# Context's projections in half as long pieces, a shorter recurrence chunk, and their phases at other gathers

## What is computed

```python
def peer_ffn(x, wq, sub_keys, u, v):           # 8 heads, top 16 of 128 x 128 experts each
    ...
        s1, i1 = lax.top_k(sc[:, :, 0], PEER_TOPK)
        s2, i2 = lax.top_k(sc[:, :, 1], PEER_TOPK)
    ...
        top_s, pos = lax.top_k(cand, PEER_TOPK)
        eidx = jnp.take_along_axis(cidx, pos, axis=-1)
        g = jax.nn.softmax(top_s, axis=-1)
        a = jax.nn.gelu(jnp.einsum('chkd,cd->chk', jnp.take(u, eidx, axis=0), xc), approximate=False)
        return jnp.einsum('chk,chkd->cd', (g * a), jnp.take(v, eidx, axis=0))
```

```python
def _gdn_scan(q, k, v, log_a, beta, s0):       # 4 heads, chunks of 128
    g = jnp.cumsum(log_a..., axis=-1)
    rel = g[..., :, None] - g[..., None, :]
    a = einsum(kc, kc) * bc * jnp.where(strict, jnp.exp(rel), 0.0)        # bc is beta
    rhs = jnp.concatenate([bc * vc, bc * jnp.exp(g)[..., None] * kc], axis=-1)
    u, wk = split(triangular_solve(a + I, rhs))
    k_tail = kc * jnp.exp(g_last - g)
    v_new = u - wk @ s;  s_next = exp(g_last) * s + k_tail^T @ v_new
    if q is not None: o = (qk * exp(rel) where incl) @ v_new + (q * exp(g)) @ s_prev
```

## Time and profile before

| | |
|---|---|
| time, median of 3 runs | 2995.73 us (2994.79 to 2996.75) |
| the profiled execution | 2992.89 us, span 2991.1 us, mean granted clock of PE 0.918 |
| busy: PE | 2436.7 us, 81% of the span |
| busy: DVE | 1598.9 us, 53% |
| busy: ACT, POOL | 836.0 us and 830.9 us, 28% each |
| gathers of the second layer | 1147 to 1890 us |
| x's features and recurrence | 1890 to 2250 us |

### The profile page before, as it was taken

How to read it: one execution, slowest core, us unless ns; L and a number is a source line. 1 busy time by engine, 2 the same in 40 slices (tenths; PEclk the granted TensorE clock), 3 DMA queues, 4 the chain that set the end, 5 groups by cost and what they waited for, 6 DMA issues and landing times.

```text
span 2991.1 us, 29479 instructions
## 1 busy us (share of the span) xinstructions
PE 2436.7 (81%) x9692; PEld 1331.3 (45%) x9692; DVE 1598.9 (53%) x3289; ACT 836.0 (28%) x2272; POOL 830.9 (28%) x723
## 2 busy tenths in 40 slices
PE   7898888888887988998897899789797786767673
PEld 3684333333333766344443455458783532222221
DVE  4556657485444636758889877556644521121111
ACT  1313333333332412343343444323110111111110
POOL 1004333343331102334444556112010112122221
PEclk9799999999999799999999999899998788888887
DMA  7029999999998126999898899612113399999994
GB/s 276 1 85 403 422 422 422 422 415 422 422 398 346 57 85 248 376 366 395 355 420 313 358 422 395 245 43 71 43 57 131 140 408 397 389 391 381 382 381 147
DMA packets 129843, 885.95 MB, mean 296 GB/s; under 512 B 23184, under 2 KB 23568, under 8 KB 31760
## 3 DMA queue, kind: packets, MB, share of 16 engines
q0 software_dynamic: 86976, 553.74, 46.0%
q1 hardware_dynamic: 42704, 330.22, 27.5%
HBM read 877.56 MB, written 37.75 MB: 306 GB/s over the span
## 4 chain that ended last, share of the span: by engine, by line
PE 46%; DMA 25%; DVE 20%; ACT 4%; issue 3%; SPq 1%; POOL 1%; DVEq 0%; ACTq 0%; POOLq 0%
PE ps L155 44%; DMA ring<-in_peer_uv,idx_u 11%; DMA ring<-in_w_gu 6%; DVE ring L1307 6%; DVE arena L76 5%; DMA ring<-in_w_down 3%; ACT arena L125 3%; PE ps L158 2%; DMA arena<-in_w_gu 2%; DMA arena<-in_w_down 1%; DVE arena L1307 1%; DVE iu L113 1%; DVE arena L109 1%; SPq L2560 1%; DVE arena L97 1%
## 5 line engine op out<-in xcount | busy, mean ns | idle before, releaser
L155 PE MATMUL ps<-ring,arena 128*128 128x512 f32 (+3 forms) x3264 | 1262.9, 653 | 281.2 <-ACT arena L125 159.9
L155 PEld LDWEIGHTS ps<-ring,arena 128*128 128x128 f32 (+2 forms) x3264 | 473.6, 180 | 957.3 <-issue 605.1
L1307 DVE CUSTOM_DVE_ANT_0 ring<-ring,h 128x1024 f32<-128x1024 f32 x448 | 563.0, 1257 | 328.3 <-DMA ring<-in_peer_uv,idx_u 294.9
L2377 POOL DMA_INDIRECT ring<-in_peer_uv,idx_u x448 | 491.5, 1097 | 754.8 <-PE ps L155 609.4
L155 PE MATMUL ps<-arena 128*128 128x128 f32 (+7 forms) x2504 | 502.8, 383 | 106.4 <-ACT arena L125 42.9
L125 ACT ACTIVATE arena<-arena 128x1 f32<-128x1 f32 (+4 forms) x1097 | 296.7, 270 | 747.6 <-DVE arena L1307 646.3
L155 PEld LDWEIGHTS ps<-arena 128*128 128x128 f32 (+3 forms) x2504 | 316.0, 193 | 263.5 <-issue 148.3
L76 DVE TENSOR_TENSOR arena<-arena,ps 128x512 f32<-128x512 f32 (+1 forms) x158 | 93.7, 593 | 446.9 <-ACT arena L125 358.6
L125 ACT ACTIVATE arena<-ps 128x512 f32<-128x512 f32 (+4 forms) x198 | 109.8, 554 | 774.1 <-PE ps L155 712.5
L155 PE MATMUL ps<-ring,hT 128*128 128x512 f32 (+2 forms) x896 | 307.0, 503 | 16.9 <-DVE hT L97 11.9
L125 ACT ACTIVATE arena<-cst,arena 128x128 f32<-128x128 f32 x512 | 205.5, 401 | 162.3 <-PE ps L155 122.0
(11 more groups left out here) (117 smaller groups left out, 1486.6 us busy)
## 6 DMA issues: line engine op xcount, KB each, us to landing
ring<-in_w_gu SPq DMA_DIRECT2D x98, 1024.0 KB, 28.5
ring<-in_w_down SPq DMA_DIRECT2D x52, 1024.0 KB, 29.8
ring<-in_w_in SPq DMA_DIRECT2D x16, 2048.0 KB, 12.6
arena<-in_w_gu SPq DMA_DIRECT2D x30, 1024.0 KB
ring<-in_w_mod SPq DMA_DIRECT2D x12, 2048.0 KB
ring<-in_peer_wq SPq DMA_DIRECT2D x8, 2048.0 KB, 8.1
ring<-in_w_o SPq DMA_DIRECT2D x6, 2048.0 KB, 11.1
ring<-in_w_gates SPq DMA_DIRECT2D x12, 1024.0 KB, 4.9
```

The costliest lines, as they stand in the source:

```text
L155: return self.e.matmul(o, lhsT, rhs, start=start, stop=stop, skip_group_check=True)
L1307: v.done(v.e.tensor_tensor_reduce(out=row, in0=row, in1=h[:, n // 128, :], scale=1.0, scalar=0.0, op0=ALU.mult, op1=ALU.add, accum_out=aa[ ...
L2377: g.e.indirect_dma_start(out=landing(n), out_offset=None, in_=d["peer_uv"], in_offset=bass.IndirectOffsetOnAxis(ap=idx_u[:, n:n + 1], axis ...
```

## The change

In words:

- `beside`: the phases of the second layer stand at n = 6, 8, ... 128, at 11, 21, ... 121, and at 139, 141, ... 237; 124 of them.
- `rows_mm` for the context's `Rk` and `Rv` yields after 4 matmuls instead of 8, and PE's `conv_features` yields in the middle of each of its two pieces. The other engines' generators have as many idle phases more.
- `gdn_chunk`: DT is made for x alone, and its product with the triangle stands behind level 2. ACT multiplies kk by beta as it copies it out of PSUM, in four operations (one a head) behind the exp of Dm, where one copied it before; DVE's product of Am with beta is gone. rk takes one product instead of two (with gc times beta, four columns) and stands behind level 1. In the tail PE waits for rv before U, where it waited for rk.

```diff
@@ -201,7 +201,7 @@
 def beside(l, n):
 
     if l:
-        return 1 if n in range(10, 130, 2) or n in range(138, 250, 2) else 0
+        return 1 if n in range(6, 130, 2) or n in range(139, 239, 2) or n in range(11, 131, 10) else 0
     return 1 if n in range(12, 246, 9) else 0
@@ -655,7 +655,7 @@
                     if name == "Rv" and not s.x:
                         yield from idle(2)
                     yield from rows_mm((s.tag, name), xT, R(area, 4), 512, ("loaded", s.tag, name), *ready,
-                                       among=among)
+                                       grain=8 if s.x else 4, among=among)
@@ -682,6 +682,8 @@
                             for k in range(8):
                                 t = pe.mm(b[:, (m - m0) * 256:(m - m0) * 256 + 256],
                                           w[:, k * 512 + m * P:k * 512 + (m + 1) * P], xT[:, k, :], k == 0, k == 7)
+                            if m == m0 and not s.x:
+                                yield
                         pe.done(t, ("ps", s.tag, name, m0), *([("used", s.tag, name)] if m0 else []))
                         yield
@@ -733,7 +735,7 @@
                     yield
                 rv, rk, kt = Dm, Am, Xm
                 b = fresh(*g, "U", among=among)
-                pe.wait_ge(*at(*g, "rk"))
+                pe.wait_ge(*at(*g, "rv"))
                 heads_mm(b, lambda sl, hd: [(XT[:, sl], rv[:, sl])], ("ps", *g, "U"))
                 b2 = fresh(*g, "W", among=among)
                 heads_mm(b2, lambda sl, hd: [(rk[:, sl], XT[:, sl])], ("ps", *g, "W"))
@@ -1377,7 +1379,7 @@
                     v.ts(xn[:, c, :], src[:, c, :], rs[:, c:c + 1], None, ALU.mult, None, (tag, c))
 
             def row_features(s):
-                yield from idle(3 * len(s.row_blocks) + (0 if s.x else 2))
+                yield from idle(3 * len(s.row_blocks) + (0 if s.x else 6))
@@ -1415,7 +1417,7 @@
                 rw = raw.rearrange("p (m t) -> p m t", m=4)
                 cvv = cv.rearrange("p (m t) -> p m t", m=4)
                 for a, name, area, f0 in kinds:
-                    for _ in range(3):
+                    for _ in range(3 if s.x else 5):
                         yield
@@ -1467,6 +1469,8 @@
                 bec = be[:, c, dr * 4:dr * 4 + 4]
                 ck = slice(c * P, (c + 1) * P)
                 g = (s.tag, dr, c)
+                Gk, Gv = s.GG[:, 0, c, :], s.GG[:, 1, c, :]
+                rv, rk, kt = Dm, Am, Xm
@@ -1476,20 +1480,17 @@
                 for hd in range(4):
                     sl = slice(hd * P, (hd + 1) * P)
                     v.ts(Dm[:, sl], GR[:, sl], gc[:, hd:hd + 1], 0.0, ALU.subtract, ALU.max, (*g, "D"))
-                for hd in range(4):
-                    sl = slice(hd * P, (hd + 1) * P)
-                    v.ts(DT[:, sl], GR[:, sl], gc[:, hd:hd + 1], 0.0, ALU.subtract, ALU.min)
+                if s.x:
+                    for hd in range(4):
+                        sl = slice(hd * P, (hd + 1) * P)
+                        v.ts(DT[:, sl], GR[:, sl], gc[:, hd:hd + 1], 0.0, ALU.subtract, ALU.min)
                 yield
                 v.wait_ge(*at(*g, "exp D"))
-                v.wait_ge(*at(s.tag, "beta", c))
                 v.tt(heads(Dm, 4), heads(Dm, 4), bc(strict, 1, 4), ALU.mult)
                 v.wait_ge(*at("out", *g, "kk"))
-                v.tt(Am, kk, Dm, ALU.mult)
-                v.tt(heads(Am, 4), heads(Am, 4), bc(bec, 2, P), ALU.mult, (*g, "A"))
-                v.wait_ge(*at(*g, "exps"))
-                v.tt(heads(DT, 4), heads(DT, 4), bc(tri, 1, 4), ALU.mult)
+                v.tt(Am, kk, Dm, ALU.mult, (*g, "A"))
                 I4 = bc(ident, 1, 4)
                 v.tt(heads(Xm, 4), heads(Am, 4), bc(C("lvl0"), 1, 4), ALU.mult)
                 v.tt(heads(Xm, 4), I4, heads(Xm, 4), ALU.subtract)
@@ -1505,11 +1506,13 @@
                         v.tt(Xm, Xm, tile_of(*g, "dX", lv)[:, :], ALU.subtract, ("out", *g, "dX", lv))
                     v.wait_ge(*at("ps", *g, "dXT", lv))
                     v.tt(XT, XT, tile_of(*g, "dXT", lv)[:, :], ALU.subtract, ("out", *g, "dXT", lv), (*g, "X", lv + 1))
-                Gk, Gv = s.GG[:, 0, c, :], s.GG[:, 1, c, :]
-                rv, rk, kt = Dm, Am, Xm
-                v.tt(heads(rv, 4), heads(Gv, 4), bc(bec, 2, P), ALU.mult)
-                v.tt(heads(rk, 4), heads(Gk, 4), bc(bec, 2, P), ALU.mult)
-                v.tt(heads(rk, 4), heads(rk, 4), bc(gc, 2, P), ALU.mult, (*g, "rk"))
+                    if lv == 1:
+                        v.wait_ge(*at(*g, "exps"))
+                        v.tt(gc, gc, bec, ALU.mult)
+                        v.tt(heads(rk, 4), heads(Gk, 4), bc(gc, 2, P), ALU.mult)
+                    if lv == 2 and s.x:
+                        v.tt(heads(DT, 4), heads(DT, 4), bc(tri, 1, 4), ALU.mult)
+                v.tt(heads(rv, 4), heads(Gv, 4), bc(bec, 2, P), ALU.mult, (*g, "rv"))
                 v.tt(heads(kt, 4), heads(Gk, 4), bc(ekt, 2, P), ALU.mult)
                 if s.x:
                     v.tt(heads(qe, 4), heads(qe, 4), s.GqT[:, :, ck], ALU.mult)
@@ -2075,7 +2078,7 @@
 
             def row_features(s):
                 for name, i, _ in s.row_blocks:
-                    yield from idle(5 if i and not s.x else 3)
+                    yield from idle(3 if s.x else 7 if i else 5)
                     X = s.Rk if name == "Rk" else s.Rv if name == "Rv" else s.Rq
@@ -2135,12 +2138,16 @@
                 gc, eg, ekt = smalls3
                 g = (s.tag, dr, c)
                 yield
-                take(kk, *g, "kk")
                 a.wait_ge(*at(*g, "D"))
                 a.act(Dm, Dm, ACT.Exp, (*g, "exp D"), scale=-1.0)
+                a.wait_ge(*at("ps", *g, "kk"))
+                for hd in range(4):
+                    a.act(kk[:, hd * P:(hd + 1) * P], tile_of(*g, "kk")[:, hd * P:(hd + 1) * P], ACT.Copy, ("out", *g, "kk"),
+                          scale=be[:, c, dr * 4 + hd:dr * 4 + hd + 1])
                 last = heads(GR, 4)[:, :, end:end + 1].rearrange("p h x -> p (h x)")
                 a.wait_ge(*at(*g, "ekt"))
-                a.act(DT, DT, ACT.Exp)
+                if s.x:
+                    a.act(DT, DT, ACT.Exp)
                 a.act(ekt, ekt, ACT.Exp)
                 a.act(eg, last, ACT.Exp)
                 a.act(gc, gc, ACT.Exp, (*g, "exps"))
@@ -2412,7 +2419,7 @@
 
             def conv_features(s, kinds, lane):
                 for a, name, area, f0 in kinds:
-                    for _ in range(6):
+                    for _ in range(6 if s.x else 8):
                         yield
```

## The result

The changed kernel takes **3006.68 us** (median of 7 runs, 3004.80 to 3009.45) against 2995.73 us before (7 runs): a ratio of 1.0039, 95% interval 1.0028 to 1.0050. The forecast was 2971 us with a range of 2948 to 2991: the time went the other way, to near the rival that ended slower (3012). The profiled execution took 3006.68 us, its span is 3004.9 us.

The account below looks back on a forecast made before the run. The prediction took DMA holes in the second layer's gathers, opened by late PE or DVE, as the prize. Gather stage -16 and x's recurrence -8.5, about -25 us, gave 2971 us, range 2948 to 2991.

Parts of the forecast that it names:

- What bounds the stage: Second layer's gathers: PE or DVE late by more than eight gathers opens DMA holes, never made up, 70 us in all.
- The term for the half pieces: Projections: each block's PE work spreads over more gathers, 0.76 us of lag draining per extra gather; -8 us.
- the slower rival: Gathers: twelve phases at odd gathers each stop the DMA 3.45 us, price 41 us, total 3012 us; chance 0.13.
- deciding price of 2.6 us: Gathers: cost per odd phase from which the slower rival decides, (25 + 6) / 12.
- Projections: -8: Projections before the first front: DMA loss shrinks by 8 us of 23.0, bounds 0 and 12.6.
- Fronts: -2.7 us each: Each chunk's front: DVE loses four subtractions (1.3 us) and two products (0.69 each), -2.7 us.
- Chunk 1: +3: First chunk's front and levels: topk and front packed into six gathers, then six phases in ten; +3 us, bounds -2.7 and +8.
- Chunk 2: -9: Second chunk's front moves to gathers 118 to 123, free of routing, ahead of the norm; -9 us, bounds 0 and -14.5.
- The prediction's own sign of being wrong in the main: Gathers: chunk 2's hole keeps its size, or holes appear at each of gathers 21, 31 and so on.
- Chunk 3: +1.4: Third chunk's front moves to gathers 163 to 169 beside three 1.4 us routing pieces: 4.1 - 2.7 = +1.4 us.
- Chunk 4: -3.2: Fourth chunk's front: DVE's excess falls from 3.9 to 1.2 us, worth -3.2 us.
- x's recurrence: -8.5: x's recurrence, after the gathers: shorter PE waits before U and A, less 1.1 for slowed rk; -8.5 us, bounds -11 and -3.
- the price of rk in level 1: x's recurrence, level 1: DVE's rk operations slow beside POOL, +0.4 us each, 1.1 us in the sum.

Follow-up runs that it names:

- no_odd: Changed kernel without phases at odd gathers before 130 (positions 2, 4, ... 128, 131, 138, 140, ... 254): 2983.8 us, 0.9962 of the kernel before.
- shifted: no_odd with twelve phases one gather earlier (11, 21, ... 121 instead of 12, 22, ... 122): 2984.0 us.
- dt_only: Kernel before, with DT left out for the context's chunks and the wait for "exps" moved to the tail: 2989.8 us, ratio 0.9986.
- pos_only: Changed kernel with the old gdn_chunk, keeping the half pieces, idle phases and 124 positions: 3013.4 us, 1.0062 of the kernel before.
- even_dt_rk: no_odd with kk as before (one ACT copy, beta's product on DVE): 2979.5 us, 0.9954 of the kernel before.
- alg_early: alg_only with its 116 positions moved up to 2, 4, ... 128 and 138, 140, ... 240: 2994.4 us.
- alg_only: Changed kernel with the new gdn_chunk, but the old projections' pieces, idle phases and 116 positions: 2985.3 us, 0.9968 of the kernel before.
- dt_rk: alg_only with kk as before (one ACT copy ahead of the exp, beta's product on DVE): 2983.9 us, 0.9972 of the kernel before.

## Why the prediction was wrong, point by point

- **What bounds the stage** was right: DMA holes where PE or DVE is late, none of them made up. Sized that way they account for the loss (+14.0 against +13.6 us).
- **The step that failed is the price of the extra phases, which the sum put at nothing in the projections.** The term for the half pieces lets every block drain over more gathers, and the sum has nothing for the odd phases that take that room back. What dismissed them was the slower rival's "Against it". It took "from 1470 to 1550 PE was busy for 77 of 80 us and the DMA never stopped" as a sign that an extra phase can hide. The row says the reverse: PE had 3 us to spare in 80. More phases ahead of gather 130 have no room in such a stretch. The changed kernel has 74 phases there, before had 60 and no_odd 64. Between no_odd and the change each of the twelve odd phases costs 1.7 us of the stage, in part by the place that it gives front 3; the rival had 3.45. Its deciding price of 2.6 us rested on a gain of 25; the rest of the change was worth 11 (no_odd), so the point was 0.9. The rival had the direction right. That its 3012 lies near 3006.7 is luck: a price twice too high was set against a gain twice too high. Its mechanism, three engines going round in one gather beside neighbours, is not shown: with a neighbour on one side and no added work there was no cost (`shifted`).
- **Projections: -8 was +4.1.** The term counted the gathers over which each block is spread. But from the first phase to the front there were 82 gathers before and 82 after, with PE 221.3 and 223.4 us busy: what the blocks gained, the room between them lost. In no_odd, where there are 98, the projections give -5.2.
- **Fronts: -2.7 us each.** For DT alone, 2.0 of the 2.7, this was right in size in the profile: the four chunks gain 8.2 us in dt_only, though the whole time gains 4.4. The 0.69 for kk's product did not come: that edit gave 0.7 us in four fronts alone, and seemed to cost 2.3 beside the others.
- **Chunk 1: +3 was +4.3**, inside its bounds, by the mechanism named: too many phases in ten gathers. The term added up PE's work over the gathers in this one place, and the projections needed the same sum.
- **Chunk 2: -9 was -1.6.** Moving the front away from the norm is not the gain that it seemed: pos_only, with the old `gdn_chunk` and the front at 120, loses 22.0 where the kernel before lost 22.2. A likely reason is that the norm and the top-k from 130 on make their hole in any case, and that the front at 120 comes behind crowded levels; no run tests it. The prediction's own sign of being wrong in the main, a chunk 2 that keeps its hole, was met. The kernels with front 2 beside the routing again lose as little (no_odd 19.9, even_dt_rk 19.4).
- **Chunk 3: +1.4 was +3.7.** Runs with the same gdn_chunk put the place alone at +5.1 (alg_early against alg_only).
- **Chunk 4: -3.2 was +3.5.** alg_only, with the front where it was, has 7.1 as before, and dt_rk 6.0: that ACT's burst ate the gain fits, but 1.1 us in one chunk is within what the clock alone moves (below). The rest came with the new place: 6.8 to 10.6 in three kernels with it or one gather beside it. What makes that spread is open, but for the clock, below.
- **x's recurrence: -8.5 was -6.0**, inside its bounds and by the waits named. The timeline of PE, first the second tail before, then the changed kernel, against the earlier trace rows:

```profile
2227.19 2.94 PE L155 MATMUL ps<-arena 128*128 128x128 f32 x24 [2.01 <-DVE arena L76]
```

```profile
2083.91 2.94 PE L155 MATMUL ps<-arena 128*128 128x128 f32 x24 [1.36 <-DVE arena L76]
...
2138.37 2.94 PE L155 MATMUL ps<-arena 128*128 128x128 f32 x24 [0.61 <-DVE arena L76]
...
2171.72 1.09 PE L158 MATMUL ps<-cst,arena 128*128 128x128 f32 x4 [7.07 <-DVE arena L76]
2174.67 1.11 PE L158 MATMUL ps<-cst,ring 128*128 128x128 f32 x4 [1.86 <-DVE ring L76]
...
2239.07 2.94 PE L155 MATMUL ps<-arena 128*128 128x128 f32 x24 [0.56 <-DVE arena L76]
```

The first tail's wait before U went from 2.06 to 0.61 in the first lane, and the second lane's (1.48) is gone; in the second tail it went from 2.01 to 0.56, and the second lane's 1.48 is gone too: 5.8, as forecast. The second front's wait for the second lane's A went from 3.31 to 1.86, the first lane's from 7.74 to 7.07: -2.1 of the -2.3 forecast. The first front gave some 0.9 of 1.5. The step that was mis-sized is the price of rk in level 1, 1.1 in the sum: the waits named shrank by 8.9 and the recurrence by 6.0, so 2.9 came back, 1.36 of it where PE now waits in level 1, as it did not, for DVE, which has the operations on rk there.

The chances erred more than the sum: 0.82 for faster rested on terms that were each argued for one engine in one place, and the one rival that looked at added work where PE was full had 0.13.

## What to carry to other kernels

Before work is moved into a stretch, add up the busy time of its tightest engine there with the new work in it, over the whole stretch and not piece by piece. Cutting pieces in half helped only where the stretch that holds them grew from 82 to 98 gathers. A window with 77 of 80 us busy and no hole is the fullest, not the safest: it holds exactly what it has. An operation that leaves one engine for another is worth what the receiving engine's followers wait for, so try such edits one by one (here two helped and the third gained nothing).

## What the hardware showed that was not expected

The idle time of a front costs PE twice, and not the same each time. The eight sums behind it, 3.60 us at 2.4 GHz, took 5.40 us in the kernel before (at 1792.37, after 4.21 us of idle time), and in the changed kernel, after 4.41 us:

```profile
1780.27 3.78 PE L155 MATMUL ps<-ring,arena 128*128 128x512 f32 x4 [4.41 <-ACT arena L125]
1783.84 2.84 PE L155 MATMUL ps<-arena 128*128 128x512 f32 x4
```

so 6.41 us from start to end. The granted clock from 1781 to 1786 was 0.52, which is the level of 1.2 GHz. Almost the same idle time was followed by 1.8 us of loss in one and 2.8 in the other. The Trainium skill, TensorE: Matmul & The Clock Gate, Part 1: The HAM clock gate, says of a kernel's start that the number of slow matmuls differs between executions with where the clock's monitor stands. If the same holds behind an idle time, two such fronts can differ by this 1.0 us for no reason in the code; these two rows fit that, but they are of two kernels, and no run here shows it apart from the code.

The same shows in stretches with the same instructions. The projections of alg_only and of dt_rk differ in nothing, but their granted clock was 0.95 and 0.97, PE was busy for 247.0 and 243.1 us, and they lost 25.9 and 24.4 us of DMA:

```profile
1154.72:1442.34 287.62, 247.03 (x707) 124.99 (x706) 199.95 (x465) 113.42 (x321) 109.44 (x99) 0.95 0.95 384
```

```profile
1155.44:1441.36 285.92, 243.05 (x708) 123.28 (x707) 199.91 (x465) 113.42 (x321) 109.48 (x99) 0.97 0.96 386
```

So a difference under 2 us in one chunk of one profile is not to be explained by an edit; the sums over four chunks and the medians carry the verdicts above.
